# Long convolution: the context's three-point butterflies go from VectorE to GpSimd, and lie beside the latent butterflies of the second half

## The reference, cut to what matters

```python
def centred_long_conv(z, h):
    L = z.shape[1]
    n = 2 * L
    y = jnp.fft.irfft(jnp.fft.rfft(z, n=n, axis=1) * jnp.fft.rfft(h, n=n, axis=0)[None], n=n, axis=1)
    return y[:, L // 2: L // 2 + L]

def hyena_mixer(u, short_w, short_b, filt, bias):
    ...
    z = v
    for n, gate in enumerate((x1, x2)):
        z = gate * (centred_long_conv(z, h[n]) + bias[n] * z)
    return z.astype(u.dtype)
```

## Time and profile before

| | |
|---|---|
| median of 3 runs | 3177.64 us |
| their range | 3174.89 to 3183.51 us |
| the profiled execution's own time | 3175.76 us |
| its span, from first to last instruction | 3174.0 us |
| mean granted clock of TensorE | 0.976 |
| busy: PE / PEld / DVE / ACT / POOL | 95% / 79% / 67% / 34% / 12% |
| the `hyena` block in the span | about 829 to 1017 us |

### The profile page before, as it was taken

One profiled execution on the slowest core, in us unless ns is written; L12 is line 12 of the kernel. 1 busy time (PEld: TensorE's weight loads), 2 busy tenths in 40 slices (PEclk: granted clock), 3 DMA queues, 4 the chain that ended last, 5 costly groups with the idle time before them and its releaser, 6 DMA issues. The chain is left out here.

```text
span 3174.0 us, 41246 instructions
## 1 busy us (share of the span) xinstructions
PE 3029.7 (95%) x15510; PEld 2513.2 (79%) x15510; DVE 2117.5 (67%) x3185; ACT 1074.1 (34%) x1405; POOL 395.4 (12%) x298
## 2 busy tenths in 40 slices
PE   7999997999868999999999999899989999999999
PEld 5788854555557899999998888787867788888887
DVE  5767655676688286777765666678784676665666
ACT  4221134444212152222221111587872433333121
POOL 1000011777422200000000000200032000000000
PEclk7999997999889999999999999999999999999999
DMA  5455400002122213444424221211114222224232
GB/s 206 142 194 175 135 3 1 1 1 108 51 93 80 107 55 111 162 160 144 157 96 168 90 90 67 87 40 43 33 43 152 73 80 79 79 89 157 91 106 106
DMA packets 102715, 305.76 MB, mean 96 GB/s; under 512 B 11879, under 2 KB 21479, under 8 KB 100552
## 3 DMA queue, kind: packets, MB, share of 16 engines
q1 hardware_dynamic: 85800, 263.76, 24.6%
q10 hardware_dynamic: 12800, 23.07, 2.0%
q0 software_dynamic: 4000, 17.37, 1.6%
HBM read 243.09 MB, written 61.08 MB: 96 GB/s over the span
## 5 line engine op out<-in xcount | busy, mean ns | idle before, releaser
L276 PE MATMUL bank<-hid_pair,w_hi 128*128 128x512 f32 (+1 forms) x1760 | 423.1, 370 | 1.8 <-DVE x L2005 1.8
L2005 DVE SCALAR_TENSOR_TENSOR x<-bank,c_mods,x 128x1024 f32<-128x1024 f32 (+1 forms) x280 | 273.7, 1007 | 195.9 <-PE bank L276 195.9
L276 PEld LDWEIGHTS bank<-hid_pair,w_hi 128*128 128x128 f32 x1760 | 307.4, 188 | 60.9 <-DVE x L2005 2.1
L256 ACT ACTIVATE w_hi<-w_raw 128x1024 fp32r<-128x1024 f32 x111 | 117.2, 1057 | 601.5 <-PE bank L276 419.5
L2469 ACT ACTIVATE slot_hi<-w_raw 128x512 fp32r<-128x512 f32 x240 | 151.1, 631 | 387.9 <-PE bank L2399 214.7
L2399 PE MATMUL bank<-t_hi,slot_hi 128*128 128x320 f32 (+1 forms) x960 | 270.5, 336 | 0.3 <-DVE c L2666 0.3
L2399 PE MATMUL bank<-t_hi,slot_lo 128*128 128x320 f32 (+1 forms) x960 | 270.4, 336 | 0.0
L2399 PE MATMUL bank<-t_lo,slot_hi 128*128 128x320 f32 (+1 forms) x960 | 270.3, 336 | 0.0
L262 DVE TENSOR_TENSOR w_lo<-w_raw,w_hi 128x1024 fp32r<-128x1024 f32 x111 | 140.2, 1264 | 173.7 <-ACT w_hi L256 173.0
L276 PE MATMUL bank<-hid_pair,w_lo 128*128 128x512 f32 (+1 forms) x880 | 240.0, 370 | 0.0
L2644 DVE TENSOR_TENSOR slot_lo<-w_raw,slot_hi 128x512 fp32r<-128x512 f32 x240 | 164.9, 688 | 65.1 <-ACT slot_hi L2469 62.0
(11 more groups left out here) (474 smaller groups left out, 5946.1 us busy)
## 6 DMA issues: line engine op xcount, KB each, us to landing
w_raw<-in_weights SPq DMA_DIRECT2D x194, 512.0 KB, 3.7
ada_rows<-in_ada_rows SPq DMA_DIRECT2D x64, 256.0 KB, 2.7
c_rows<-in_ada_rows SPq DMA_DIRECT2D x64, 256.0 KB, 2.8
hid_raw<-hid_scratch SPq DMA_DIRECT2D x11, 1280.0 KB, 5.7
hid_scratch<-c SPq DMA_DIRECT2D x40, 320.0 KB, 3.3
ada_early<-in_ada_early SPq DMA_DIRECT2D x48, 256.0 KB, 3.1
hid_raw<-hid_scratch SPq DMA_DIRECT2D x11, 1024.0 KB, 5.1
hid_scratch<-c SPq DMA_DIRECT2D x40, 256.0 KB, 4.2
```

The source lines that it names most:

```text
L256: e.activation(k.w_hi[s][:, :], k.w[s][:, :], ACT.Copy).then_inc(k.split_hi[s], 1)
L276: mm = e.matmul(out[:, c:c + m], w[:, c1:c1 + P], x[:, c:c + m], start=(first and kk == 0 and n == 0), stop=(last and kk == kt - 1 and n = ...
L2005: ins = e.scalar_tensor_tensor(out=k.x[:, m, a:b], in0=k.acc[s][:, a:b], scalar=gate(m, n), in1=old[:, m, a:b], op0=ALU.mult, op1=ALU.add)
```

## The change

There are three edits.

`butterfly_ctx` is put in instructions that GpSimd is given too: the fused multiply and add for `y[:, 1]` becomes a multiply by -0.5 (TENSOR_SCALAR) and an add in place (TENSOR_TENSOR). It has four instructions instead of three, wherever it is called.

In `hyena` the calls leave VectorE's stream and stand at the head of each order in GpSimd's, ahead of all `add_terms` of that order. GpSimd first waits for the latent butterfly of half 0 (`h_xh_c` lies where `h_zt` of half 0 was), and for each half for the copy that makes `h_zt_c`. It has its own `Steps` and raises a new semaphore, `y_xc`, that `forward_ctx` waits for. Each of the four instructions waits for the one before it.

VectorE goes from the products of half 0 to those of half 1 with nothing between them. `xh_ready` is raised twice in an order, not four times, and the counts follow.

```diff
 def butterfly_ctx(e, steps, x, y):
     steps(e.tensor_tensor(y[:, 0], x[:, 0], x[:, 1], ALU.add))
-    steps(e.scalar_tensor_tensor(out=y[:, 1], in0=x[:, 1], scalar=-0.5, in1=x[:, 0], op0=ALU.mult, op1=ALU.add))
+    steps(e.tensor_scalar(y[:, 1], x[:, 1], -0.5, None, ALU.mult))
+    steps(e.tensor_tensor(y[:, 1], y[:, 1], x[:, 0], ALU.add))
     steps(e.tensor_scalar(y[:, 2], x[:, 1], -S3, None, ALU.mult))
...
+    xc_ready, c_steps_sem = k.stage_sem("y_xc"), k.stage_sem("y_xc_steps")
...
-                e.wait_ge(xh_ready, 4 * order + 2)
+                e.wait_ge(xh_ready, 2 * order + 2)
...
-                    e.wait_ge(xh_ready, 4 * order + 3 + h)
+                    e.wait_ge(xc_ready, 2 * order + 1 + h)
                     e.wait_ge(sp_read, spectrum(order, "lat", h, 3) + 1)
...
                 for pos in range(NL):
                     read = product_terms(order, "lat", 0, pos)
                 e.wait_ge(sp_read, read)
-                for h in range(2):
-                    e.wait_ge(zt_read, order * TURNS + 9 + h)
-                    butterfly_ctx(e, steps, zt_c[h], xh_c[h])
-                    e.sem_inc(xh_ready, 1)
                 for pos in range(NL):
                     read = product_terms(order, "lat", 1, pos)
...
+            c_steps = Steps(e, c_steps_sem)
             for order in range(2):
+                e.wait_ge(xh_ready, 2 * order + 1)
+                for h in range(2):
+                    e.wait_ge(zt_read, order * TURNS + 9 + h)
+                    butterfly_ctx(e, c_steps, zt_c[h], xh_c[h])
+                    e.sem_inc(xc_ready, 1)
                 for h in range(2):
                     for pos in range(NL):
                         add_terms(order, "lat", h, pos)
```

More of the change, by code:

```diff
@@ L1793, in _ @@
                 turn_ctx(order, 0)
-                e.wait_ge(xh_ready, 4 * order + 1)
+                e.wait_ge(xh_ready, 2 * order + 1)
                 for pos in range(4):
```

## The result

The changed kernel took 3181.96 us (median of 22 runs, 3179.89 to 3188.03), the kernel before 3177.58 beside it (22 runs). The profiled execution took 3182.48, its span is 3180.7, and its mean granted clock 0.975. Two lines come in ahead, so VectorE's products are now L1874, L1875 and L1877, GpSimd's adds L1982, and the context's butterfly L581 to L584.

A forecast was written before the change was run, and what follows sets the result against it. VectorE's latent butterflies, then TensorE's transforms, were taken to bound the block. Per order 3.4 us of clash plus 0.84 of clock, twice, gave 8.5 us on the median 3177.64: 3186.1 us, range 3180.0 to 3190.5.

The forecast's parts named there:

- Within 0.3%: Whole kernel: a change of at most 9.5 us, indistinguishable from none; given a chance of 0.63.
- no-turn rival: Second latent butterfly: GpSimd gets in only after it, VectorE undelayed, pos 6 late; 3.8 us in all, 3181.4; chance 0.14.
- The emptied 3.9 us count nothing: Between VectorE's products of both halves: removing 3.9 us per order saves nothing, since TensorE runs unbroken for 38 us.
- nor do the spectra: Filter spectra in `even_in`: VectorE's fourth butterfly instruction, 1.8 us in all, is covered by TensorE and counts nothing.
- Half 0's group takes turns with the latent butterfly: VectorE's second latent butterfly: half 0's four GpSimd context-butterfly instructions delay it by 1.7 us.
- the rule of length less 0.18: At the butterflies: each GpSimd instruction delays VectorE by its own time less 0.18; add 0.57, multiply 0.27 us.
- fail upward: Sign of failure: the prediction would be too low if the multiply took over 0.7 us on GpSimd.
- Half 1's group takes turns too: Second latent butterfly, from 848.7 us: half 1's four GpSimd instructions all fit before its end, delaying VectorE 1.7 us.
- port term: Both halves' GpSimd instructions clashing with VectorE's second latent butterfly: 3.4 us per order, bounds 2.7 to 4.8.
- Behind the butterflies no wait: GpSimd's adds after the butterflies: done by about 852.3, first add asked for at 855.1, so nothing waits.
- The clock, 0.84 more per order: TensorE's restart before pos 4: a pause of 7.0 us lengthens the low clock, 0.84 us per order, bounds 0 to 1.0.

The follow-up runs named there:

- e1b: Changed kernel with both halves' context butterflies on GpSimd moved behind half 0's adds; 3179.25 us, ratio 1.0011.
- e2b: Kernel before with only the helper changed: four-instruction context butterfly, still on VectorE at its old place; 3176.89 us, ratio 1.0002.
- e5b: Changed kernel with half 0's context butterfly left early on GpSimd and half 1's moved behind half 0's adds; 3181.28 us, ratio 1.0017.
- e3b: Changed kernel with each context butterfly on GpSimd replaced by one memset of the same tile; 3178.40 us, ratio 1.0004.
- e4b: Changed kernel with both context butterflies on GpSimd waiting for half 1's copy; 3183.34 us, ratio 1.0022.
- e6b: Changed kernel with half 1's context butterfly early on GpSimd and half 0's moved behind half 0's adds; 3176.58 us, ratio 0.9997.
- e10: Changed kernel, half 0's group held until VectorE's 8th (order 0) or 17th (order 1) butterfly instruction, half 1's behind the adds; 3177.00 us, ratio 1.0001.
- e11: Changed kernel with half 1's group early, a small memset right ahead of it, half 0's behind the adds; 3176.04 us, ratio 0.9998.
- e8: Changed kernel with 21 spare matmuls in TensorE's pause before pos 4 of half 0, each order; 3177.76 us, ratio 1.0003.
- e12: Changed kernel, half 0's group held until VectorE's 1st (order 0) or 2nd (order 1) butterfly instruction, half 1's behind the adds; 3180.59 us, ratio 1.0013.
- e7b: Changed kernel with half 0's context butterfly formed twice on GpSimd; 3187.75 us, ratio 1.0035.

## Why the prediction was right, and where its steps were not

The forecast was +8.5 us; the timed runs say +4.4 by the medians and some 5.7 by the ratio, the profiled block +5.67. "Within 0.3%" was right; the sum is half again to twice what was measured. The time falls nearest to the no-turn rival's 3181.4, but that is chance: its terms (no delay of VectorE, 1.9 us of waiting before pos 6 in each order) are not those of the trace.

- **The emptied 3.9 us count nothing, nor do the spectra.** Right, shown by e1b and e2b. TensorE's run is no shorter with VectorE free.
- **Half 0's group takes turns with the latent butterfly.** Right, shown by e5b and e3b. The add's delay was forecast at 0.57 and is 0.52 to 0.57. The multiply's was 0.27, from a length of 0.45 less 0.18. It is 0.19, while the instruction lasts 0.85 alone. The length was nearly twice the forecast, and the rule of length less 0.18 doesn't hold for it; the prediction said that it would fail upward if the multiply took over 0.7, and it didn't. The two errors nearly cancelled, by luck: 1.7 forecast, 1.5 measured.
- **Half 1's group takes turns too.** This step failed. The prediction weighed the rows of 1.2 us, in which turns are seen, against VectorE's short instructions, and held that those too follow each other without a gap. In both orders, and in e4b, e6b, e10 and e11, the add was shut out. With this the port term is 1.5 and not 3.4 us per order. The rival of no turn had the mechanism right for this half; its price, 1.9 per order with both groups shut out, showed as waits of 2.88 and 2.76 in e4b, since eight instructions with four multiplies of 0.85 last 7 us and not the 4.8 and waits that it reckoned. (It also put pos 6 at 856.6, which the trace before has at 856.77.)
- **Behind the butterflies no wait.** Wrong on VectorE (2.01 us before the third product), right on TensorE, by a cover that the prediction didn't name: the low clock. e8 takes it away and a wait of 0.9 us per order appears.
- **The clock, 0.84 more per order.** Right in kind: 0.90 and 1.42 in the profiled execution, whose first window after the pause shows it, to be read against the 3.41 us at 0.53 in the earlier trace rows:

```profile
851.95:857.12 5.17, 5.17 (x12) 4.16 (x13) 3.16 (x8) 0.00 (x0) 4.56 (x5) 0.51 0.42 176
...
946.38:952.52 6.14, 6.14 (x15) 4.88 (x16) 3.94 (x10) 0.00 (x0) 5.53 (x6) 0.50 0.36 151
```

  The 1.42 lies above the bound of 1.0, and the pauses were 5.18 and 4.63, not 7.0. And the term doesn't go by the pause. With the same seams the runs were +0.91 and -0.25 in e5b and +1.0 and -0.19 in e12; e7b had +1.19 and +0.14 behind pauses of 8.05 and 9.06; e11 had +1.37 and +0.72 behind 3.96 and 4.57 (3.64 and 3.60 before). In each of these the difference is what the stretch at the lower level loses, worked out as in the prediction, to within 0.1 us: that stretch lasted from 2.72 us (e5b, order 1, granted clock 0.50) to the 6.14 above. What sets its length was not tried. So this term is to be had as a range, -0.3 to 1.4 per restart, and one profiled execution doesn't give its mean.
- **Not foreseen:** 0.35 us of issue before order 1's last context product.

Put together, 2 x 1.5 for the turns, 0.35 for the issue and a clock term between 0.7 (e5b) and 2.3 (after) give 4.0 to 5.7, which is what the blocks show; the medians and the ratio, 4.4 and 5.7, agree with it.

## What to carry to other kernels

Before work goes from VectorE to GpSimd, look at whether the source engine is what anybody waits for at the place it leaves, and what VectorE is doing at the place where it lands: beside operands in PSUM, or if it only writes SBUF, it was free here, and beside VectorE instructions with two SBUF inputs each GpSimd add that was let in cost some 0.54 us of whoever waits for VectorE. If such work must lie there, its price depends on when it asks: let in, it delays VectorE; shut out, it delays all that is queued behind it on GpSimd. Behind the adds (e1b) the move cost 0.4 us by the trace, and gained nothing either. And read a pause of TensorE as two costs, the pause and the restart behind it, of which the second can be bought off with spare matmuls (14 in each of two pauses of 3.6 us gave 3.3 us in the block and 4.2 by the medians).

## What was not expected of the hardware

- **GpSimd can be shut out for as long as VectorE's stream lasts.** An add of 0.72 us took 6.88 in e10. The Trainium skill, "SBUF — State Buffer", section "Who interferes with whom", says that issue order decides who blocks. The trace agrees for half 0's group, where each delays the other in turn, and differs here: by the starts of the records, 19 of VectorE's 28 instructions began after GpSimd's add of 843.50 in e10, and all of them passed it. The measurement decides.
- **VectorE's TENSOR_SCALAR gives no turn and is delayed too.** In e10 two of them (0.28 us each) ran while GpSimd's add waited. In e7b one lasted 0.81 us beside an add that got its turn:

```profile
846.20 1.00 POOL L583 TENSOR_TENSOR h_xh_c<-h_xh_c,h_zt_c 128x256 f32<-128x256 f32 x1
...
846.54 0.81 DVE L546 TENSOR_SCALAR h_xh<-h_bt 128x256 f32<-128x256 f32 x1
```

- **A GpSimd TENSOR_SCALAR is slower than a TENSOR_TENSOR of the same size** (0.85 against 0.72 us for 128x256 in f32), and delays VectorE less (0.19 against 0.52 to 0.57).
